# The wait of TensorE's pause placed directly behind the signalling matmul, and two pauses left in the expert stage

## The reference, cut to what matters

```
h = rmsnorm(x);  proj = h @ w_in                  # first block: 52 columns of 128 each
... gating, delta rule, cross attention ...;      x = x + mixed @ w_out
h = rmsnorm(x);  proj = h @ w_in_2                # second block: 80 columns of 128
... two attentions ...;                           x = x + (merged @ w_out_2)
h = rmsnorm(x);  q = h @ w_query;  scores against 2 x 128 keys per head
top 16 of each half, top 16 of their sums, softmax -> gates over 16384 experts
x = x + (gates * gelu(h @ expert_u.T)) @ expert_v # all 16384 experts, dense
out = rmsnorm(x)
```

## Time and profile before

| what | value |
|---|---|
| median of 3 runs | 3000.95 us |
| the three runs | 2997.36, 3000.95, 3005.54 us |
| the profiled execution: its own time | 3004.29 us |
| its span (first to last instruction) | 3002.5 us |
| granted TensorE clock, mean over the span | 0.987 |
| TensorE matmul busy | 2906.8 us, 97%, 24182 matmuls |
| POOL busy | 2289.1 us, 76% |
| ACT busy | 1312.0 us, 44% |
| DVE busy | 1063.2 us, 35% |

### The profile page before, as it was taken

How to read it: one execution, slowest core, us unless ns; L and a number is a source line. 1 busy time by engine, 2 the same in 40 slices (tenths; PEclk the granted TensorE clock), 3 DMA queues, 4 the chain that set the end, 5 groups by cost and what they waited for, 6 DMA issues and landing times.

```text
span 3002.5 us, 58955 instructions
## 1 busy us (share of the span) xinstructions
PE 2906.8 (97%) x24182; PEld 2865.0 (95%) x24182; DVE 1063.2 (35%) x1558; ACT 1312.0 (44%) x1547; POOL 2289.1 (76%) x925
## 2 busy tenths in 40 slices
PE   7999979999999988999999999999999999999998
PEld 7999979899999987999999999999999999999998
DVE  6113365353000025225698981403104040033322
ACT  6355542554534343444443664343433334333333
POOL 6787730588878852888799548888888888889986
PEclk9999989999999998999999999999999999999999
DMA  6445410344545530555454555564564645655553
GB/s 241 169 175 184 162 62 0 113 176 175 194 169 196 182 140 31 193 195 183 156 182 177 215 224 210 182 219 173 192 215 180 224 168 196 219 192 205 211 188 118
DMA packets 85829, 524.37 MB, mean 175 GB/s; under 512 B 8672, under 2 KB 23136, under 8 KB 24544
## 3 DMA queue, kind: packets, MB, share of 16 engines
q1 hardware_dynamic: 68400, 489.38, 45.5%
q10 hardware_dynamic: 17328, 33.56, 3.0%
HBM read 504.03 MB, written 18.87 MB: 174 GB/s over the span
## 4 chain that ended last, share of the span: by engine, by line
PE 51%; POOL 23%; issue 20%; DVE 5%; POOLq 0%; ACT 0%; DVEq 0%; ACTq 0%
PE banks L1345 51%; POOL wlo L404 23%; DVE oh L1273 2%; DVE oh L1269 1%; DVE hidden L1283 1%; POOLq L403 0%; DVE T L800 0%; PE banks L1455 0%; DVE hid_lower L1316 0%; DVE dec L1007 0%; POOLq L398 0%; DVE picks L1254 0%; DVE at__97 L1015 0%; DVE qkv L967 0%; ACT expr L605 0%
## 5 line engine op out<-in xcount | busy, mean ns | idle before, releaser
L404 POOL TENSOR_TENSOR wlo<-raw,whi 128x1024 fp32r<-128x1024 f32 x920 | 2284.4, 2504 | 661.6 <-ACT whi L427 660.7
L427 ACT ACTIVATE whi<-raw 128x1024 fp32r<-128x1024 f32 x916 | 943.0, 1055 | 763.2 <-PE banks L1345 755.8
L1345 PE MATMUL banks<-xhi,whi 128*128 128x256 f32 x4928 | 681.8, 281 | 7.1 <-ACT xhi L508 7.0
L1345 PE MATMUL banks<-xhi,wlo 128*128 128x256 f32 x4928 | 678.4, 280 | 6.2 <-POOL wlo L404 6.2
L1345 PE MATMUL banks<-xlo,whi 128*128 128x256 f32 x4928 | 682.6, 281 | 1.9 <-DVE xlo L807 1.9
L1345 PEld LDWEIGHTS banks<-xhi,whi 128*128 128x128 f32 x4928 | 622.1, 189 | 9.3 <-issue 7.8
L1345 PEld LDWEIGHTS banks<-xlo,whi 128*128 128x128 f32 x4928 | 623.4, 189 | 5.8 <-DVE xlo L807 2.5
L1345 PEld LDWEIGHTS banks<-xhi,wlo 128*128 128x128 f32 x4928 | 620.9, 189 | 7.6 <-POOL wlo L404 7.6
L878 DVE TENSOR_TENSOR X<-banks,X 128x256 f32 (+1 forms) x112 | 47.5, 424 | 768.9 <-PE banks L1345 768.9
L1345 PE MATMUL banks<-hid_lower,whi 128*128 128x256 f32 x2048 | 285.5, 282 | 2.4 <-DVE hid_lower L1316 2.4
L1345 PEld LDWEIGHTS banks<-hid_lower,whi 128*128 128x128 f32 x2048 | 261.1, 190 | 3.7 <-DVE hid_lower L1316 2.6
(11 more groups left out here) (352 smaller groups left out, 2156.8 us busy)
## 6 DMA issues: line engine op xcount, KB each, us to landing
raw<-in_w_exp SPq DMA_DIRECT2D x256, 1024.0 KB, 4.8
raw<-in_w_in SPq DMA_DIRECT2D x132, 1024.0 KB, 4.8
raw<-in_w_out SPq DMA_DIRECT2D x32, 1024.0 KB, 4.8
raw<-in_w_br SPq DMA_DIRECT2D x16, 1024.0 KB, 4.8
raw<-in_w_q SPq DMA_DIRECT2D x16, 1024.0 KB, 4.8
gates<-gst ACTq DMA_DIRECT2D x16, 1024.0 KB, 4.7
gch<-gates ACTq DMA_DIRECT2D x7, 2048.0 KB, 12.8
raw<-in_w_kv SPq DMA_DIRECT2D x8, 1024.0 KB, 9.5
```

What stands on the lines that cost most here:

```text
L404: pool.tensor_tensor(wlo[:, s, :, :], raw[:, j, h * HALF:(h + 1) * HALF, :], whi[:, s, :, :].bitcast(F32), ALU.subtract).then_inc(lo_ready, 1)
L427: act.activation(whi[:, (2 * j + h) % 4, :, :], raw[:, j, h * HALF:(h + 1) * HALF, :], ACT.Copy).then_inc(hi_ready, 1)
L1345: return nc.tensor.matmul(o, lhsT, rhs, start=start, stop=stop, **k)
```

## The change

`pause` is one call now: the last matmul of the first pass counts up `beat`, and the wait stands directly behind it, ahead of the first weight load and matmul of the next pass (of lower x, or of lower weights in the paired segment). `segment` takes a parameter `paused`. In the experts only up 0 and down 1 (the down-projection with e == 1) keep their pause; up 1, down 0, up 3 to up 7 and down 2 to down 7 have none. The 19 pauses ahead of the experts stay.

```diff
-            def pause(k, z):
-                if k == HALF - 1:
-                    z.then_inc(beat, 1)
-                    beats[0] += 1
-                elif k == 0:
-                    pe.wait_ge(beat, beats[0])
+            def pause(z):
+                z.then_inc(beat, 1)
+                beats[0] += 1
+                pe.wait_ge(beat, beats[0])
...
                         if paused and h == 0 and k == HALF - 1:
-                            pause(k, z)
+                            pause(z)
...
                             z = mm(oo, whi[:, s0 + h, k, :], lo[:, tile(k), :], start=False, stop=stop and k == HALF - 1)
-                            if paused and h == 0 and k == 0:
-                                pause(k, z)
...
-            def segment(u0, n, paired=False, hi=xhi, lo=xlo, fresh=None, between=None):
+            def segment(u0, n, paired=False, hi=xhi, lo=xlo, fresh=None, between=None, paused=True):
                 for j in range(2):
-                    unit_body(u0, j, hi, lo, u0 // 2, paired, fresh if j == 0 or paired else None, between if j == 0 else None, j == 1)
+                    unit_body(u0, j, hi, lo, u0 // 2, paired, fresh if j == 0 or paired else None, between if j == 0 else None, paused and j == 1)
...
                 elif kind == "up":
-                    segment(u0, KT, fresh=split(L_EXP) if e == 0 else None)
+                    segment(u0, KT, fresh=split(L_EXP) if e == 0 else None, paused=e == 0)
                 elif e < EXPERT_CHUNKS - 1:
-                    segment(u0, KT, False, *gated(e), gates_of(e))
+                    segment(u0, KT, False, *gated(e), gates_of(e), paused=e == 1)
                 else:
-                    segment(u0, KT, False, *gated(e), gates_of(e))
+                    segment(u0, KT, False, *gated(e), gates_of(e), paused=False)
```

## The result

The changed kernel takes 2988.92 us in the median of 17 runs (2954.18 to 2994.25), the kernel before, beside it, 3004.01 us (17 runs, 2992.74 to 3010.32). The ratio is 0.9928, with a 95% interval from 0.991 to 0.9946: faster by 0.7%. Forecast were 2941 us and a gain of 2%; the time lies inside the stated range, but the gain is a third of the forecast one. It is where the rival "one release, one result" put it, at 2987. Three of the 17 runs are apart from the others, at 2954.18, 2959.22 and 2960.65; they are part of the 0.7%, for the two medians alone differ by 0.5%. Ratios in this document leave out the runs of a kernel that lie over 1.5% above its fastest (none of these 34), so where the kernel before has runs near 2934 and near 3003 us, as further down, the ratio stands against the lower level.

A forecast was written before the change was run, and what follows sets the result against it. TensorE, busy 97%, was taken as the bound: number of matmuls times their start-to-start distance. 3004.3 - 44.7 - 14.7 - 2.5 + 2.1 = 2944.5 us, as a median 2941; whole range 2922 to 2993.

The forecast's parts named there:

- one release, one result: Rival for all pauses: the weight load's release instant decides, so fast always turns slow; median 2987 us, chance 0.31.
- The price of the pause: At each pause: 0.21 us today, 0.11 more with the moved wait; +2.1 us for 19 kept, -2.5 us for 12 removed.
- 6.9 + 0.4: Down 0 and up 3: 6.9 us if their 1536 matmuls turn fast; removed pauses were priced at 0.21 us each.
- Up 0 to up 2: First up-projections of the experts: no gain, since DVE covers them; at most 6.9 us from up 0 and up 1, not summed.
- Spacing behind the experts' gates: From 1817 us to the end: all 9936 matmuls turn from slow to fast spacing, -44.7 us; lower bound nothing.
- The eight of eight: TensorE's waits for POOL at full clock: all eight were followed by the fast spacing, used as evidence against slow.
- POOL keeps up: Experts' segments without pauses: a subtraction takes 2533 ns against 2718 ns for half a unit, leaving 0.19 us.
- Spacing ahead of the experts: Nine long slow windows before the experts: between nothing and 29.4 us to gain; half taken, -14.7 us.
- one miss costs one stretch: Ahead of the experts: each slow stretch hangs on its own pause, so a failure loses only that stretch.
- The 13 of 13: Pauses in the profile before that found the fast spacing: all 13 left the slow one.
- slower: Rival: the kept pauses break what is fast now, up to 3306 matmuls, +14.9 us; median 3015 us, chance 0.05.
- the spacing doesn't follow the pause: Rival for all segments: only the pause's price changes, 3003.9 us, as a median 3001; chance 0.06.

The follow-up runs named there:

- e1_down1_off: The changed kernel without the pause in down 1, so that up 0's is the only one left in the experts; 2978.51 us, ratio to before 1.0094.
- r2_after: The changed kernel, unaltered, run once more on another chip beside the kernel before; 2981.59 us, ratio to before 1.0172.
- section 1: First batch of experiments, on one chip: four variants of the changed kernel with pauses taken away or put back; the kernel before took 2951.19 us there.
- e2_up3_on: The changed kernel with one pause more, in up 3; 2984.53 us, ratio to before 1.0113.
- e3_all_on: The changed kernel with all 34 pauses, so only the moved wait is left of the change; 2970.69 us, ratio to before 1.0062.

## Why the prediction was right or wrong

**Right.** The two spacings of 113.25 and 117.75 ns, that each holds itself, and that their mixture makes up most of the difference between versions: every trace of the study is made of them. The price of the pause: the gap behind the signal is 0.33 us in place of 0.12, as worked out. Down 0 and up 3 came back fast, and with their pauses gone the stretch took 8 us less; 6.9 + 0.4 were expected. Up 0 to up 2, counted at nothing, took 340 and 339 us: DVE's cover holds.

**Wrong: "Spacing behind the experts' gates", -44.7 us.** The step took as its nearest rows those in which TensorE had run empty and then started on a weight load, as they went to fast without exception, and called emptiness the common property. What they had in common, as far as the runs tell, was that each began at an instant of its own, most of which give fast: over all traces about four of five waits for POOL at full clock left fast. The pause begins at a fixed instant after its own signal, the same with or without a matmul in flight, and in executions of the first kind, the recorded one among them, that is one that leaves slow: 64 of 64, 12 of them in the recorded trace. Measured were the 6.9 of the first two segments and nothing behind down 1. The eight of eight were also too small a sample: e1_down1_off and r2_after show waits for POOL that set slow.

The same step had a second fault, its condition that fast survives ten segments since "POOL keeps up". The 2533 ns were a mean over short and long subtractions; from up 3 to up 7 five in each up-projection take 3.4 us, against the 2.72 us of half a unit. In e1_down1_off, where down 1 has no pause, fast ended at such a subtraction in up 3, and the kernel took 2978.51 us, not 2951. So without down 1's pause the 44.7 us would not have come either.

The rival had the mechanism, the alternation and the number (2987 against 2988.92); I gave it 0.31 on the argument that slow would need a special instant. It needed exactly one, and a pause that repeats itself meets it each time. That its time fits to 2 us is in part luck: the attention stage took 5.5 us that were in no sum.

**Mis-sized: "Spacing ahead of the experts", -14.7 us.** Two segments turned fast, some 3.5 us each, so 7; "one miss costs one stretch" was right as a rule, but the misses are not independent: each fast segment makes the next slow.

**Not foreseen: the kind of execution.** The sum, and all rivals, took the trace of before as the kernel's one behaviour. The 13 of 13 were a property of that execution. In the second kind the same pauses leave fast, the kernel before takes 2934 us and the change costs 1.7%. This is the rival "slower", with the wrong mechanism: not pauses that break what is fast, but pauses taken out (down 2 to down 7, up 4 to up 7) that would have repaired what a wait for POOL broke, together with a moved wait that leaves slow what it finds slow. So the recorded gain of 0.7% is the answer for executions of the first kind, of which, by their times of 2993 to 3010 us, all 17 runs of the kernel before there were.

**The rival "the spacing doesn't follow the pause"**, near 3001 us, is out: the spacing changed at all 21 pauses. The Trainium skill, "TensorE: Matmul & The Clock Gate", section "Back-to-back issue gap", gives N / 2.4 + 2.5 ns at full clock as the gap of an isolated matmul, which makes 109.2 ns for 256 columns, an estimate from that formula. For a stream in which each matmul has its weight load, as here, it says that both set the spacing, with figures for 128 and 512 columns only. The traces show 113.25 and 117.75 ns for this stream at one clock, and the kernel before alone takes from 2924 to 3010 us.

**Open.** What makes an execution of one kind or the other: it went mostly by chip, but one chip gave both to the same kernel, and one execution changed within itself. What the instant is measured against. Why the kernel before took 2935 to 2959 us in its 12 runs on the chip of section 1, between the two levels, while e2_up3_on and e3_all_on were profiled there in the first kind: none of the 12 has a trace. And the three runs of the changed kernel near 2957 us, which have no trace; that down 1's pause found slow in them, and so left the tail fast, fits their distance of 32 us from the median, but is only argued.

## What to carry to other kernels

When a stream of equal matmuls shows two start-to-start distances at one clock, list for every stop in it what spacing stood before and behind, by what released it, and do this in several executions before you price anything: one trace can show a rule that holds 13 of 13 times and is reversed on the next chip. Where one engine must keep up with another, compare its longest instructions with the slack, not their mean. A stop that a program imposes on itself did the same each time within an execution (one of them apart), so try offsets for it, and keep it often enough to repair what irregular waits break; taking repairs away looks free in a trace in which they do nothing. Compare before with before on more than one chip when the gain in question is of the order of one per cent.

## What the hardware showed that I had not expected

- One program takes 2934 or 3003 us (2.3%), at a mean granted clock of 0.985 and 0.987, because most of its 22,080 unit matmuls start 113.25 ns apart in the one case and 117.75 in the other.
- A matmul of 16 weight columns and 4 moving columns, put behind a wait, changes the spacing of the thousands of matmuls behind it; one of 2 columns does not (7 of 7 fast against 11 of 11 slow, both in executions of the first kind).
- The first weight load behind a wait on TensorE's own matmul starts 0.33 us after that matmul's start, with a matmul between the two (before) and without one (after).
- A wait that had been met before, written as a second one, moved nothing: 332 ns with it and without it.
- POOL's subtraction of the same 128x1024 took 3.4 us in place of 2.4 five times in each up-projection from up 3 to up 7 (before), at times when DVE worked on the hidden values.
